# Split queries of the expert search, tokens parked in DRAM, two dots of the late heads moved

## The reference, cut to what matters

```python
def peer(h, w_query, sub_keys, expert_u, expert_v):
    def block(xb):
        q = (xb @ w_query).reshape(t, PEER_HEADS, 2, PEER_HALF)      # 8 heads x 2 x 128
        scores = jnp.einsum('thpd,hpnd->thpn', q, sk)                # against 128 keys per side
        s_val, s_idx = lax.top_k(scores, PEER_TOPK)                  # 16 of 128
        ...                                                          # 16 experts per head and token
        act = jax.nn.gelu(jnp.einsum('thkd,td->thk', expert_u[expert], xb))
        return jnp.einsum('thk,thkd->td', gate * act, expert_v[expert])
x = x + peer(rmsnorm(x, ln_ffn[l]), ...)
```

## Time and profile before

| | us |
|---|---|
| median of 3 runs | 2827.73 (2824.94 to 2829.92) |
| profiled execution | 2825.03 |
| its span, first to last instruction | 2823.2 |
| TensorE busy | 2795.2 (99%) |
| VectorE busy | 2334.7 (83%) |
| ScalarE busy | 1045.3 (37%) |
| mean granted TensorE clock | 0.998 |

### The profile page before, as it was taken

How to read it: one execution, slowest core, us unless ns; L and a number is a source line. 1 busy time by engine, 2 the same in 40 slices (tenths; PEclk the granted TensorE clock), 3 DMA queues, 4 the chain that set the end, 5 groups by cost and what they waited for, 6 DMA issues and landing times.

```text
span 2823.2 us, 40525 instructions
## 1 busy us (share of the span) xinstructions
PE 2795.2 (99%) x15010; PEld 1572.8 (56%) x15010; DVE 2334.7 (83%) x4390; ACT 1045.3 (37%) x1382; POOL 747.1 (26%) x518
## 2 busy tenths in 40 slices
PE   9999999999999999999989999999999999999999
PEld 5455555556666444444467775555566664444444
DVE  6954899997888899999733568999978888999996
ACT  2253222234555333333342442323345553333333
POOL 0000233321111454544100002333301115545450
PEclk9999999999999999999999999999999999999999
DMA  4213678767998999999512246878679979999993
GB/s 159 89 47 144 240 274 294 277 245 274 312 309 283 391 394 399 392 399 396 207 64 90 77 155 242 315 255 310 246 268 316 312 294 396 395 400 392 397 397 147
DMA packets 214838, 776.05 MB, mean 275 GB/s; under 512 B 15508, under 2 KB 101912, under 8 KB 194744
## 3 DMA queue, kind: packets, MB, share of 16 engines
q1 hardware_dynamic: 50096, 416.89, 38.7%
q0 software_dynamic: 73728, 268.47, 25.8%
q10 hardware_dynamic: 90888, 89.14, 9.2%
HBM read 681.90 MB, written 92.54 MB: 274 GB/s over the span
## 4 chain that ended last, share of the span: by engine, by line
PE 92%; DVE 2%; ACT 2%; issue 1%; DMA 1%; PEld 1%; DVEq 0%; PEldq 0%; POOL 0%; ACTq 0%; SPq 0%
PE ps L1966 31%; PE ps L1896 12%; PE ps L1897 12%; PE ps L1895 12%; PE ps L1869 8%; PE ps L1483 3%; PE ps L1571 2%; PE ps L1948 2%; PE ps L1947 2%; PE ps L1520 1%; PE ps L1521 1%; PE ps L1524 1%; PE ps L1905 1%; PEld ps L1966 1%; PE ps L1667 1%
## 5 line engine op out<-in xcount | busy, mean ns | idle before, releaser
L1966 PE MATMUL ps<-arena 128*128 128x512 bf16 x4584 | 990.7, 379 | 3.8 <-ACT arena L760 2.5
L521 POOL DMA_INDIRECT arena<-in_ur,arena x256 | 348.8, 1362 | 1556.0 <-DVE arena L1188 934.2
L1966 PEld LDWEIGHTS ps<-arena 128*128 128x128 bf16 x4584 | 448.1, 98 | 545.2 <-issue 3.0
L1161 DVE TENSOR_TENSOR arena<-arena 128x1024 bf16<-128x1024 f32 x512 | 611.5, 1220 | 116.9 <-ACT arena L760 94.2
L1897 PE MATMUL ps<-xnh,arena 128*128 128x384 bf16 x2048 | 667.6, 326 | 0.0
L1896 PE MATMUL ps<-xnl,arena 128*128 128x384 bf16 x2048 | 667.5, 326 | 0.0
L1895 PE MATMUL ps<-xnh,arena 128*128 128x384 bf16 x2048 | 667.4, 326 | 0.0
L760 ACT ACTIVATE arena<-arena 128x1024 bf16<-128x1024 f32 x512 | 524.2, 1048 | 120.7 <-PE ps L1966 97.3
L521 POOL DMA_INDIRECT arena<-in_v,arena x256 | 397.4, 1552 | 402.6 <-DVE x_res L1197 342.2
L1197 DVE SCALAR_TENSOR_TENSOR x_res<-arena,x_res 128x1024 f32<-128x1024 f32 x256 | 328.6, 1283 | 21.1 <-issue 0.9
L786 ACT ACTIVATE arena<-ps 128x384 f32<-128x384 f32 x256 | 125.6, 491 | 563.8 <-PE ps L1897 563.7
(11 more groups left out here) (247 smaller groups left out, 2534.1 us busy)
## 6 DMA issues: line engine op xcount, KB each, us to landing
arena<-in_v SPq DMA_DIRECT2D x64, 2048.0 KB, 10.4
arena<-in_u SPq DMA_DIRECT2D x62, 2048.0 KB, 10.4
h_scratch<-arena ACTq DMA_DIRECT2D x60, 768.0 KB
arena<-h_scratch SPq DMA_DIRECT2D x60, 768.0 KB, 8.6
arena<-gate_scratch SPq DMA_DIRECT2D x64, 640.0 KB, 6.9
arena<-in_wmix SPq DMA_DIRECT2D x14, 2048.0 KB, 7.8
gate_scratch<-xnT ACTq DMA_DIRECT2D x10, 2048.0 KB
gate_scratch<-arena ACTq DMA_DIRECT2D x10, 2048.0 KB
```

The lines of the kernel that those rows point to most:

```text
L521: pool.indirect_dma_start(ring[n % NBUF], None, ur_d[L] if g < P else vr_d[L], at).then_inc(gat_in[n % NBUF], 16)
L1161: dve.tensor_tensor(lo[:, s], raw[s // TPG][:, s % TPG], hi[:, s], ALU.subtract).then_inc(lo_ready, 1)
L1966: last = pe.matmul(ps[:, 2 + 2 * tt + dh], c, v[:, TPG * s + q, dh * 512:(dh + 1) * 512], start=start and c is ch and v is hi, stop=stop a ...
```

## The change

The queries become three passes over split operands. ScalarE rounds the query weights of a head (`query_high`, two instructions), VectorE makes their rest in place (`query_low`, two instructions), and the normed tokens are split too (`query_rest`). The token rest `x_rest` (2 MB) lies where the residual `x` lies, so `x` is written to DRAM (`x_keep`) tile by tile before, and SyncE loads it back after the last head's queries. Each late head loses two dots after its top-16; the gate stage has three dots for four tiles where it had two.

```diff
+                sp.wait_ge(q_done, PH * (L + 1))
+                for tt in range(TT):
+                    sp.dma_start(x[:, tt], x_keep[tt]).then_inc(x_back, 16)
                 with sp.Fori(PH - 1, 2 * PH - 1) as h:          # SyncE: loads of groups 16 on
...
                 act.activation(std[:, tt:tt + 1], ss[:, tt:tt + 1], ACT.Sqrt, ...).then_inc(norm_std, 1)
+                if k % 2:
+                    act.dma_start(x_keep[tt], x[:, tt]).then_inc(x_kept[tt], 16)
...
+            def query_high(L, h):                                # ScalarE
+                act.wait_ge(wq_in, 16 * (PH * L + h + 1))
+                for p in range(2):
+                    at = slice(4 * p, 4 * p + 4)
+                    act.activation(wq_hi[h][:, at], wq[:, at], ACT.Copy).then_inc(q_high, 1)
...
+                    if n % RING == 5 and n < NK // 2 - RING:     # in ScalarE's loop over tiles
+                        query_high(L, n // RING + 1)
...
+            def query_rest(k, tt):                               # VectorE, within norm_split
+                at = slice(tt * P, (tt + 1) * P)
+                dve.wait_ge(xt_low, TT * k + tt + 1)
+                dve.drain()
+                if tt:
+                    src = xs[:, tt].rearrange("p (k t) -> p k t", t=P)
+                    dve.tensor_copy(x_hi[:, :, at], src)
+                    dve.wait_ge(x_kept[tt], 16 * (k // 2 + 1))
+                    dve.drain()
+                    dve.tensor_tensor(x_rest[:, tt], src, x_hi[:, :, at].bitcast(F32), ALU.subtract).then_inc(xt_rest, 1)
+                    return
...
+            def query_low(L, h):                                 # VectorE
+                for p in range(2):
+                    at = slice(4 * p, 4 * p + 4)
+                    dve.wait_ge(q_high, 2 * (PH * L + h) + p + 1)
+                    dve.tensor_tensor(wq_lo[:, at], wq[:, at], wq_hi[h][:, at].bitcast(F32), ALU.subtract).then_inc(q_low, 1)
...
                     ahead(RING * h + 12)
+                    if h + 1 < PH:
+                        query_low(L, h + 1)
                     dots(1 if late else 0)
...
-                    dots(3 if late else 0)                       # after the top-16 of head h
+                    dots(1 if late else 0)
...
-                        dots(n % 2)                              # gate stage
+                        dots(int(n % 4 != 0))
...
+                            dve.wait_ge(x_back, 16 * TT * (L + 1))   # before the first sum
...
+                def queries(h, s, tiles):                        # TensorE, bank, at, cols_at as before
+                    pe.wait_ge(q_high, 2 * (PH * L + h + 1))
                     for kd in range(KD):
-                        last = pe.matmul(ps[:, 2 + s, at], wq[:, kd, s * P:(s + 1) * P], xnT[:, kd, at], ...)
+                        pe.matmul(bank, wq_hi[h][:, kd, cols_at], x_hi[:, kd, at], start=kd == 0, stop=False)
+                        pe.matmul(bank..., wq_hi[h][:, kd, cols_at], x_rest[:, tiles, kd], start=False, stop=False)
+                    pe.wait_ge(q_low, 2 * (PH * L + h + 1))
+                    for kd in range(KD):
+                        last = pe.matmul(bank, wq_lo[:, kd, cols_at], x_hi[:, kd, at], start=False, stop=kd == KD - 1)
```

More of the change, by code:

```diff
@@ L95, in build @@
     vr_d = [v.rearrange("n g (q d) -> (n g q) d", q=TPG) for v in v_d]
+    x_keep = nc.dram_tensor("x_keep", [TT, P, D], F32).ap()
     skew_d = nc.dram_tensor("skew_scratch", [HEADS, P, REL], F32).ap()
@@ L211, in build @@
         o_lo = rounded("o_lo", 12288, KD, T)
+        x_rest = rounded("x_rest", ARENA + KD * T + KD * TD, TT, KD, P)
+        wq_lo = rounded("wq_lo", A_X, KD, 2 * P)
+        wq_hi = [rounded("wq_hi0", A_X + 2304, KD, 2 * P)] + [rounded("wq_hi1", A_GR, KD, 2 * P)] * (PH - 1)
         def x_low(kd):
@@ L289, in build @@
         xt_rest = sem("xt_rest")
+        q_high = sem("q_high")
+        q_low = sem("q_low")
+        x_kept = [sem(f"x_kept{tt}") for tt in range(TT)]
+        x_back = sem("x_back")
         w_high = sem("w_high")
@@ L551, in norm_low @@
                 for kd in range(KD // 2):
-                    dst = x_hi if k == 2 else xnT
-                    last = act.activation(dst[:, kd, tt * P:(tt + 1) * P], ps[:, turn_bank(k, tt), kd * P:(kd + 1) * P], ACT.Copy,
+                    dst = xnT if k == 0 else x_hi
+                    dst = xs[:, tt, kd * P:(kd + 1) * P] if k % 2 and tt else dst[:, kd, tt * P:(tt + 1) * P]
+                    last = act.activation(dst, ps[:, turn_bank(k, tt), kd * P:(kd + 1) * P], ACT.Copy,
                                           scale=cols[:, C_GAIN + KD * k + kd:C_GAIN + KD * k + kd + 1])
@@ L887, in norm_high @@
                     at = (kd - KD // 2) * P
-                    dst = x_hi if k == 2 else xnT
-                    last = dve.tensor_scalar(dst[:, kd, tt * P:(tt + 1) * P], ps[:, turn_bank(k, tt) + 1, at:at + P],
+                    dst = xnT if k == 0 else x_hi
+                    dst = xs[:, tt, kd * P:(kd + 1) * P] if k % 2 and tt else dst[:, kd, tt * P:(tt + 1) * P]
+                    last = dve.tensor_scalar(dst, ps[:, turn_bank(k, tt) + 1, at:at + P],
                                              cols[:, C_GAIN + KD * k + kd:C_GAIN + KD * k + kd + 1], None, ALU.mult)
@@ L934, in project_out @@
                         weights_lo(SPLIT0 + 7, range(2 * step, 2 * step + 2))
+                    if step == 2:
+                        query_low(m, 0)
                     if step and out_steps[m][step - 1][1] == 1:
@@ L1451, in turned @@
                     pe.wait_ge(xt_high, 2)
+                if k % 2 and tt == 2:
+                    pe.wait_ge(xt_rest, TT * (k - 1) + 1)
                 if k % 2 and tt >= 2:
@@ L1754, in mixer1 @@
                 pe.wait_ge(xt_high, TT * 2 + 2)
-                pe.wait_ge(xt_rest, 2)
+                pe.wait_ge(xt_rest, TT + 2)
                 q_banks = unit_bank(), unit_bank()
@@ L1760, in mixer1 @@
                 all_turned(2)
-                pe.wait_ge(xt_rest, TT)
+                pe.wait_ge(xt_rest, 2 * TT)
                 for h in range(2):
@@ L1865, in peer @@
                 T0 = STREAM * L
-                def queries(s, at):
-                    for kd in range(KD):
-                        last = pe.matmul(ps[:, 2 + s, at], wq[:, kd, s * P:(s + 1) * P], xnT[:, kd, at],
-                                         start=kd == 0, stop=kd == KD - 1)
-                    return last
[L1873 to L1877, removed]
+                def queries(h, s, tiles):
+                    at = slice(tiles.start * P, tiles.stop * P)
+                    cols_at = slice(s * P, (s + 1) * P)
+                    bank = ps[:, 2 + s, at]
+                    pe.wait_ge(q_high, 2 * (PH * L + h + 1))
+                    for kd in range(KD):
+                        pe.matmul(bank, wq_hi[h][:, kd, cols_at], x_hi[:, kd, at], start=kd == 0, stop=False)
+                        pe.matmul(bank.rearrange("p (a t) -> p a t", t=P), wq_hi[h][:, kd, cols_at], x_rest[:, tiles, kd],
+                                  start=False, stop=False)
+                    pe.wait_ge(q_low, 2 * (PH * L + h + 1))
+                    for kd in range(KD):
+                        last = pe.matmul(bank, wq_lo[:, kd, cols_at], x_hi[:, kd, at], start=False, stop=kd == KD - 1)
+                    return last
+                halves = slice(0, TT // 2), slice(TT // 2, TT)
+                pe.wait_ge(xt_rest, 2 * TT * L + 2)
+                queries(0, 0, halves[0])
                 turned(2 * L + 1, TT - 1)
[L1879 to L1882, removed]
+                queries(0, 1, halves[0])
+                pe.wait_ge(xt_rest, 2 * TT * L + TT)
+                queries(0, 0, halves[1])
+                queries(0, 1, halves[1]).then_inc(q_done, 1)
                 pe.wait_ge(xn_split, DT * (L + 1))
@@ L1914, in peer @@
                     tile(h * RING, 0)
-                    pe.wait_ge(wq_in, h * 16 + 16 * (PH * L + 1))
                     for s in range(2):
-                        last = queries(s, slice(0, T))
+                        last = queries(h, s, slice(0, TT))
                     last.then_inc(q_done, 1)
```

12 lines of the change are left out of this document (9 added, 3 removed).

## The result

The changed kernel takes 2842.26 us (median of 4 runs, 2842.11 to 2846.55), the kernel before 2828.13 beside it: 1.0055 times as long, 95% interval 1.0043 to 1.0068. The profiled execution took 2842.32, its span is 2840.5 against 2823.2. The forecast was slower, 2836, range 2824 to 2845. The medians differ by 14.1 us, the spans by 17.3, since the profiled execution of the kernel before ran 3.1 us under the median of its group.

The account below looks back on a forecast made before the run. TensorE was taken to bound the kernel, busy 2795.2 of 2823.2 us, with VectorE almost equally long in the heads. Per layer -8.35 + 0 + 7.0 + 1.8 + 2.7 = +3.15; two layers plus 1.9 give +8.2: 2836, range 2824 to 2845.

Parts of the forecast that it names:

- head 0: Head 0's queries in quarters: 2.0 us saved, set against waits for the token rest; taken as 0 a layer.
- heads 1 to 7: Later heads' queries: head 1 gains 2.85 us, head 2 1.35, heads 3 to 7 0.83 each; 8.35 a layer.
- stall at tile 60 and clock: TensorE waits 7.0 us a layer for tile 58's gelu behind the late group 16 load; lowered clock adds 1.8.
- group 19, tile 72: Late `lo` of tile 71 delays the group 19 load, so TensorE waits at tile 72: 2.7 us a layer.
- layer 1's last projection: Tile 1's copy and subtraction stand ahead of tile 2's norm, delaying its transposes: 1.9 us, once.
- Three passes, VectorE's balance: Queries take 10.88 us for 13.73; VectorE's added subtractions balance its lost dots, so it sets late heads at 45.9 us.
- Reload: Loading `x` back ahead of group 16 makes that load land 17.5 us after the first issue; stall 7.0 a layer.
- crowded row: Profile row of loads amid gathers: 1152 + 2048 KB in 14.5 us, so 18.5 for the reload's 4096 KB.
- two rivals of a lesser stall: At tile 60: reload stalls 5.0 us, 2826, chance 0.22; or is nearly hidden, stall 3.3, 2820, chance 0.10.
- Gate stage: One more dot per four tiles fits VectorE's waits, 0.7 us to spare; rival that it fills up: 2848, chance 0.10.
- Clock: Lower TensorE clock after the tile 60 gap costs 1.8 us a layer; shorter stalls in the heads leave it alone.

Follow-up runs that it names:

- Experiments 4: The changed kernel with the two dots of each late head put back into the head stage: 2873.78 us (1.0161).
- 10: The kernel of experiment 9 with one more dot of each late head moved to the gate stage: 2794.43 us, 0.9880.
- 12: All five edits on the changed kernel (those of experiments 1, 3, 9, 10, 11 and the weight rests one place earlier): 2790.12 us, 0.9874.
- Experiment 1: The changed kernel with the loads of groups 16 and 17 issued ahead of the wait for head 7's queries and the reloads: 2826.49 us, 0.9994.
- experiment 2: The changed kernel with the expert stage's first loads held until the last store to x_keep has landed: 2845.64 us (1.0065).
- experiment 11: The kernel of experiment 9 with the third passes of both half heads done last in heads 1 to 7: 2806.95 us, 0.9927.
- experiment 9: The changed kernel with group loads earlier, weight rests earlier, token rest last, and layer 1's last-projection residual declared new ahead of the split: 2805.07 us, 0.9922.
- experiment 5: The kernel before with only the two dots of each late head moved to the gate stage: 2830.0 us, 1.0004.
- experiment 3: The changed kernel with what needs the last token rest put last in head 0: 2840.95 us (1.0051).

## Why the prediction was right, and where it was off

The outcome (slower) and the time (2842.3 in 2824 to 2845, and in the forecast's own range of 2831 to 2843) held. In spans the sum said +8.2 and +17.3 was measured, in medians +14.1. Measured parts are changes in when TensorE reaches a mark (end of queries, start of the gate stage), both traces from the start.

| term | predicted | layer 0 | layer 1 |
|---|---|---|---|
| head 0 | 0 (-1 to +3) | +7.5 | +5.3 |
| heads 1 to 7 | -8.35 | -8.2 | -8.35 |
| stall at tile 60 and clock | +8.8 | +10.1 | +8.9 |
| group 19, tile 72 | +2.7 | 0 | 0 |
| layer 1's last projection | +1.9 | | +3.5 |
| all else, start and `peer_v` stage | 0 | -0.6 | -0.9 |

The measured terms make 8.8 + 8.45 = 17.3.

- **Three passes, VectorE's balance: right.** Heads are 45.77 apart (45.9 predicted). Head 1 gives the full 2.8, the rest that is made during it stalls head 2's third pass by 1.47 and 1.44 (1.5 predicted), and heads 2 to 7 give 0.7 to 1.1 each. Experiments 4, 10 and 12 show it from both sides: two dots added cost 2.25 a head, one dot less gives TensorE's pace back in all but the last two heads. The number of subtractions times their row was what mattered.
- **Reload: right in mechanism, close in size.** Group 16 came 18.8 us after the first issue; the crowded row gave 18.5, and 17.5 was taken. Experiment 1 removes the term whole. The two rivals of a lesser stall needed 15.5 and 13.8.
- **The step that failed: "I take 0 for head 0".** Its mechanism was named (the third quarter needs the token rest, behind the store, beside 4 MB of loads), but its size was set with the bounds -1 to +3 and no row of a crowded store. It measured 7.5 and 5.3. The store took 10.52 us beside the loads and 2.61 alone (experiment 2). Part of it is again the clock, 0.50 after the gap. I had applied the crowded row to the reload and not to this store: 4.6 MB at the rate of the earlier trace rows take over 20 us, and VectorE asks for the store 4.5 us after its issue (its cast to `x_hi` ends at 254.5). That row would have overstated the wait, which was 6.14, but would have kept it from being nothing. That the range held is luck: with the next term as it was predicted, the time would have been some 2848.
- **Follow-up at group 19: absent.** 5.4 us of the sum were not there. Counted from the end of head 7's scores (598.4), the `lo` of tile 71 ended at 51.5 (50.5 predicted), but the load was used 9.1 us after its issue, where 12 was taken. The gelu for tile 72 was made at 62.3 (64.2 predicted), and TensorE reached that tile only at 65.2, not 61.6: it came after a stall of 7.8 and its clock, and the sum had left the clock's 1.8 out of this arrival. ScalarE waited for the load and TensorE did not:

```profile
659.25 1.06 ACT L775 ACTIVATE arena<-arena 128x1024 bf16<-128x1024 f32 x1 [2.56 <-DMA arena<-in_u]
660.22 0.47 ACT L809 ACTIVATE arena<-ps 128x384 f32<-128x384 f32 x1
```

  The chain of causes was not wrong: experiment 11 met it one group earlier, at tile 68. VectorE's lag died at the entry, as said, where it waited 6.0 us and had waited 9.07.
- **Layer 1's last projection: mechanism right, 3.5 for 1.9.** The wait before the third transposes is 2.46 where it was 0.56, which is the 1.9 predicted to the tenth. What was left out is the rest: a wait of 0.64 before the second transposes, and the clock, which is below 1.00 behind the longer wait and was at 1.00 in this place before.

```profile
1652.43 1.81 PE L1516 MATMUL ps<-const,arena 128*128 128x128 f32 x8 [2.46 <-DVE arena L907]
```

```profile
1650.00:1655.00 5.00, 2.57 (x11) 2.41 (x12) 2.24 (x6) 2.33 (x7) 0.00 (x0) 0.76 0.27 108
1655.00:1660.00 5.00, 5.00 (x22) 4.06 (x20) 4.15 (x6) 0.00 (x0) 0.00 (x0) 0.90 0.00 0
```

  The split stands ahead of the signal on which ScalarE starts its squares; experiment 9 moved the signal and took 3.6 back, clock included.
- **Gate stage: no cost,** as said (experiment 5).
- **Clock.** The sum's 1.8 a layer at tile 60 fits: windows of 0.65 and 0.67 there. That "the stalls of 1.5 to 2 in the heads cost only themselves" is true of this trace, but not in general: in experiment 3, with waits of up to 1.91, four heads ran partly below full clock. The Trainium skill, "TensorE: Matmul & The Clock Gate", section HAM oscillation, says that gaps between bursts throttle the clock again; these traces agree for the gaps of 5.5 to 7.8 us in the changed kernel and for the one of 2.46, and only for a few of the many of under 2 us.

Left open: the 1 us or less gained in each `peer_v` stage, and which of the shorter waits lower the clock.

## What to carry to other kernels

A saving on the busiest engine is worth only what the second one leaves: work out both per period, and move work, not waits. Here the three passes brought all of their 2.8 us a head as soon as three dots a head, not two, had left VectorE. A transfer put into a full queue costs by who stands behind it: 2 MB of reloads cost 9 to 10 us a layer ahead of a load and nothing behind it; price each new wait on a transfer, a store's too, by a crowded row. And an edit that gains little alone may be worth more once the next limit is gone, so try them together: the token rest last brought at most 1.3 us alone and 4.6 behind two others. The third passes last brought nothing alone and some 2 at the end, which the medians by themselves do not prove.

## What the runs showed of the hardware

- A store of 512 KB took 2.61 us alone and 10.52 beside some 4.5 MB of loads that were issued from 2 us before it on, on another queue.
- Waits of 1.44 to 1.78 us of TensorE left the granted clock at 1.00 in all twelve heads of the changed kernel that had one; waits of 1.75 to 1.91 in experiment 3 gave windows of 0.66 to 0.72 in four heads, at 2 us more each, and two further waits of 1.76 and 1.91 did not.
- The time up to head 0's queries differs between profiles, by up to 8 us: 247.4 in the changed kernel, 252.4 in kernel 10. In this pair it is the clock, long before any query: kernel 10's is lowered early on, while the changed kernel's is 1.00 in the same windows. The shares missing from 1.00 make 5.1 us, and the difference is 5.0. What lowers it in one execution and not in another is not shown.

```profile
10.00:15.00 5.00, 3.99 (x20) 3.26 (x21) 3.96 (x14) 4.86 (x18) 0.00 (x0) 0.73 1.19 291
15.00:20.00 5.00, 5.00 (x11) 3.19 (x12) 2.04 (x6) 0.18 (x1) 0.00 (x0) 0.50 1.12 402
20.00:25.00 5.00, 5.00 (x23) 4.23 (x22) 0.57 (x3) 1.00 (x4) 0.00 (x0) 0.75 0.92 370
```
